# Fetched expert rows gated and added on GpSimd instead of VectorE, in a two-block transformer kernel

## The reference, cut to what matters

```python
def moe_swiglu(h, router, w_gate, w_up, w_down):
    ...
    vals, idx = lax.top_k(probs, TOP_K)
    wts = vals / jnp.sum(vals, axis=-1, keepdims=True)
    gates = jnp.einsum('tk,tke->te', wts, jax.nn.one_hot(idx, N_EXPERTS, dtype=jnp.float32)).astype(h.dtype)
    out = jnp.zeros_like(ht)
    for e in range(N_EXPERTS):
        out = out + gates[:, e:e + 1] * swiglu(ht, w_gate[e], w_up[e], w_down[e])
    return out.reshape(bsz, seq, d)
```

## Time and profile before

| | |
|---|---|
| Median of three runs | 1274.33 us (1272.78 to 1274.46) |
| The profiled execution, its time | 1270.87 us |
| Its span in the profile | 1269.1 us |
| Granted TensorE clock, mean over the span | 0.999 of full speed |
| TensorE busy | 1236.7 us (97%) |
| VectorE busy | 1001.9 us (79%) |
| ScalarE busy | 844.2 us (67%) |
| GpSimd busy | 39.0 us (3%), 47 instructions |

### The profile page before, as it was taken

How to read it: one execution, slowest core, us unless ns; L and a number is a source line. 1 busy time by engine, 2 the same in 40 slices (tenths; PEclk the granted TensorE clock), 3 DMA queues, 4 the chain that set the end, 5 groups by cost and what they waited for, 6 DMA issues and landing times.

```text
span 1269.1 us, 18118 instructions
## 1 busy us (share of the span) xinstructions
PE 1236.7 (97%) x5924; PEld 1015.1 (80%) x5924; DVE 1001.9 (79%) x1397; ACT 844.2 (67%) x1218; POOL 39.0 (3%) x47
## 2 busy tenths in 40 slices
PE   7999999999998999999999999999997999999998
PEld 6878888888777787888788888888786877888887
DVE  6577555556977899999999999999999787766664
ACT  5656444446755788888888888888886587544442
POOL 0000000000100000000000000000100121000000
PEclk9999999999999999999999999999999999999999
DMA  9744555554233699999999999989998433455540
GB/s 357 276 162 170 195 187 181 194 198 166 68 133 133 257 369 378 363 361 370 362 376 372 357 376 374 375 344 370 375 422 301 166 140 115 165 182 196 175 156 34
DMA packets 48196, 325.22 MB, mean 256 GB/s; under 512 B 5416, under 2 KB 6704, under 8 KB 9872
## 3 DMA queue, kind: packets, MB, share of 16 engines
q1 hardware_dynamic: 44704, 316.40, 66.4%
q10 hardware_dynamic: 2752, 5.77, 1.2%
q0 software_dynamic: 688, 2.36, 0.5%
HBM read 318.74 MB, written 5.77 MB: 256 GB/s over the span
## 4 chain that ended last, share of the span: by engine, by line
PE 89%; DVE 5%; ACT 3%; issue 1%; POOL 0%; DMA 0%; SPq 0%; DVEq 0%; ACTq 0%
PE bank L431 25%; PE bank L433 25%; PE bank L432 25%; PE bank L1135 4%; PE bank L1136 2%; DVE wl L1812 2%; PE bank L495 2%; ACT wh L1193 1%; PE bank L842 1%; PE bank L467 1%; PE bank L697 1%; PE bank L1134 1%; PE bank L696 1%; DMA x<-x_dram 0%; DVE xt L1832 0%
## 5 line engine op out<-in xcount | busy, mean ns | idle before, releaser
L1812 DVE TENSOR_TENSOR wl<-raw,wh 128x1024 fp32r<-128x1024 f32 x598 | 714.5, 1219 | 180.3 <-ACT wh L1193 170.3
L1193 ACT ACTIVATE wh<-raw 128x1024 fp32r<-128x1024 f32 x598 | 630.5, 1058 | 278.2 <-PE bank L433 239.5
L431 PE MATMUL bank<-wh,xt 128*128 128x512 f32 (+2 forms) x1026 | 406.4, 396 | 6.6 <-DVE xt L1832 2.5
L433 PE MATMUL bank<-wh,xt 128*128 128x512 f32 (+2 forms) x1026 | 397.1, 387 | 0.0
L432 PE MATMUL bank<-wl,xt 128*128 128x512 f32 (+2 forms) x1026 | 396.5, 386 | 0.0
L431 PEld LDWEIGHTS bank<-wh,xt 128*128 128x128 f32 x1026 | 193.1, 188 | 45.5 <-DVE xt L1832 3.2
L433 PEld LDWEIGHTS bank<-wh,xt 128*128 128x128 f32 x1026 | 192.9, 188 | 40.3
L432 PEld LDWEIGHTS bank<-wl,xt 128*128 128x128 f32 x1026 | 193.4, 189 | 36.1
L431 PE MATMUL bank<-wh,hth 128*128 128x512 f32 x472 | 186.4, 395 | 1.0 <-DVE htl L1880 0.4
L433 PE MATMUL bank<-wh,htl 128*128 128x512 f32 x472 | 184.7, 391 | 0.0
L432 PE MATMUL bank<-wl,hth 128*128 128x512 f32 x472 | 184.3, 390 | 0.0
(11 more groups left out here) (304 smaller groups left out, 822.6 us busy)
## 6 DMA issues: line engine op xcount, KB each, us to landing
raw<-weights_dram SPq DMA_DIRECT2D x299, 1024.0 KB, 5.2
expert_results<-wide ACTq DMA_DIRECT2D x7, 512.0 KB
x<-x_dram SPq DMA_DIRECT2D x2, 512.0 KB, 7.3
wide<-bias_scratch ACTq DMA_DIRECT2D x8, 128.0 KB, 4.0
out_dram<-x SPq DMA_DIRECT2D x4, 256.0 KB, 2.0
fixed<-fixed_dram SPq DMA_DIRECT2D x1, 536.0 KB, 11.2
bias_scratch<-act ACTq DMA_DIRECT2D x2, 256.0 KB, 8.5
bias_scratch<-hbuf ACTq DMA_DIRECT2D x2, 256.0 KB, 14.9
```

What stands on the lines that cost most here:

```text
L431: mm(o, lh, wh[:, wi, sl], start=start, stop=False)
L433: return mm(o, ll, wh[:, wi, sl], start=False, stop=stop)
L1193: A(wh[:, c % SPLIT, 0:n], raw[:, (c // 2) % RAW, (c % 2) * UNIT:(c % 2) * UNIT + n], ACT.Copy).then_inc(hi_done, 1)
L1812: V.tensor_tensor(wl[:, c % SPLIT, 0:n], raw[:, (c // 2) % RAW, (c % 2) * UNIT:(c % 2) * UNIT + n], f32(wh[:, c % SPLIT, 0:n]), ALU.subtra ...
```

## The change

The four fused operations of `add_fetched` on VectorE go, with the wait for the fetch and the hooks (`near_end`) by which they were called. On GpSimd, right behind the four indirect DMAs, eight operations of 128x1024 come in: four multiply the fetched rows by their gates in place, and four add them to x, one after the other for the same half of x. They count the semaphore `ob_rs` up to eight. VectorE waits for that count before `add_scattered`, and the waits of `scaled_ob` are raised by the same eight.

```diff
@@ gpsimd, behind the four indirect DMAs
+            pool.wait_ge(sem("fetched"), 64)
+            for choice in range(2):
+                for t in range(NT):
+                    gate = small[:, 68 + 2 * choice + t:69 + 2 * choice + t]
+                    g.tensor_scalar(fetched(choice, t), fetched(choice, t), gate, None, ALU.mult).then_inc(sem("ob_rs"), 1)
+            for choice in range(2):
+                for t in range(NT):
+                    pool.wait_ge(sem("ob_rs"), 2 * NT if choice == 0 else 2 * NT + t + 1)
+                    g.tensor_tensor(x[:, t, :], x[:, t, :], fetched(choice, t), ALU.add).then_inc(sem("ob_rs"), 1)
             norm_rs("attn2")
@@ vector, ffn
-                if near_end:
-                    near_end(0)
...
-                        if near_end:
-                            near_end(1)
@@ vector
-            def add_fetched(t):
-
-                dv.wait_ge(sem("fetched"), 64)
-                for choice in range(2):
-                    gate = small[:, 68 + 2 * choice + t:69 + 2 * choice + t]
-                    link(V.scalar_tensor_tensor(out=x[:, t, :], in0=fetched(choice, t), scalar=gate, in1=x[:, t, :],
-                                                op0=ALU.mult, op1=ALU.add))
-
             def add_scattered():
 
+                dv.wait_ge(sem("ob_rs"), 4 * NT)
                 for n in range(2):
...
-            expert(NE - 1, 2, near_end=add_fetched, leave=leave_moe)
+            expert(NE - 1, 2, leave=leave_moe)
@@ vector, scaled_ob
-                dv.wait_ge(sem("ob_rs"), h + 1)
+                dv.wait_ge(sem("ob_rs"), 4 * NT + h + 1)
```

More of the change, by code:

```diff
@@ L1853, in out_proj, with ffn @@
                 turned_lo(tag, range(4, 8), 6)
-            def ffn(tag, c0, nf, U, loops, width, nd, i0, f0=0, nt=NT, early=None, late=None, done=0, leave=None, middle=None, near_end=None):
+            def ffn(tag, c0, nf, U, loops, width, nd, i0, f0=0, nt=NT, early=None, late=None, done=0, leave=None, middle=None):
                 nj = width // P
```

## The result

The changed kernel is slower. Its median is 1275.61 us (18 runs, 1273.65 to 1281.09) against 1272.72 us of the kernel before (18 runs, 1271.12 to 1274.91); the ratio is 1.0026 with a 95% interval of 1.0018 to 1.0033. Its profiled execution took 1275.02 us, with a span of 1272.9. The prediction was 1280.6 us, or +6.3 us. The sign was right and 1275.61 lies in the range, but only about half of the forecast slowdown came: 2.9 us between the medians, 3.3 by the ratio. The absolute figure misses by 5.0 us. Some 1.6 of that is the base: the prediction started from the median of three runs, 1274.33, and that of eighteen is 1272.72.

The account below looks back on a forecast made before the run. TensorE, busy 97% of the span, was taken as the bound. New idle time of 10.7 us plus 1.5 us of low clock less 5.9 us for the removal gave +6.3 us, 1280.6 us; range 1268 to 1287.

Parts of the forecast that it names:

- What bounds the kernel: Whole kernel: TensorE busy 97% of the span; near the change it waits 4.6 us for VectorE's line 1870.
- what the removal gives: End of the mixture: without VectorE's four additions, 4.4 us of TensorE waiting and 1.5 us of slow clock go, 5.9 together.
- Two-sided hold: VectorE's splits beside GpSimd: each engine's operation holds the other's, a GpSimd operation for its whole length; 13.8 us held.
- H: Time GpSimd's eight operations hold VectorE's splits, from about 930 us on: 13.8 us, ends 9.2 and 24.
- (b): Rival on VectorE's splits: held, but only 5 to 10 us; net -2.5 to +2.5 us, middle 1274.3; chance 16%.
- What is absorbed: 930 to 955 us: 3.1 us of held time doesn't reach TensorE, so 10.7 come out as idle time.
- the low clock's cost: TensorE's products behind its last wait for VectorE run at 1.2 GHz instead of 2.4; 1.5 us, counted once.
- The margin of 1.3 us: VectorE's lead over TensorE: first additions put 2.59 us in and 1.26 came out, so 1.3 us is absorbed.
- H - 7.5: General net change in us for held time H; the change breaks even at 7.5 us held.
- When it runs: GpSimd's new work: last fetch lands at 930 us, work lasts until 953, VectorE's new wait costs nothing.
- (a): Rival on VectorE's splits: GpSimd waits for them but they aren't held; only the removal counts, -5.9 us, 1268.4; chance 20%.
- (c): Rival on GpSimd: served only when VectorE rests, so VectorE's new wait stalls TensorE; +7.5 us, 1281.8; chance 6%.

Follow-up runs that it names:

- the eight additions: Kernel before with eight further additions of 128x1024 on GpSimd in expert 0's steps; 1290.95 us, ratio 1.0136.
- the spread kernel: Kernel before with VectorE's four additions spread out, one behind line 1880 of each of steps 3 to 6 of expert 7; 1271.01 us, ratio 0.9988.
- the run for their own durations: Kernel before with one multiplication and one addition of 128x1024 on GpSimd near the start; multiplication 2.89 us, addition 2.36 us.

## Why the prediction was right or wrong

**What bounds the kernel, and what the removal gives: right.** 5.9 us were forecast, 5.7 shown by the run without additions, and the 0.2 us of waiting left over were 0.54.

**Two-sided hold: right.** It decided the sign. The rows of short operations showed only that GpSimd waits for splits; that splits wait for GpSimd was taken on argument and on the rule of the Trainium skill, and the eight additions show it. The Trainium skill, "SBUF — State Buffer", section "SBUF: two separate sides", has the one that starts first keep the shared interface for the whole instruction. That is nearly borne out for additions: held 1.9 to 2.1 us of the 2.36 that one takes. It isn't for multiplications: by this rule 2.89 us would be held each time, and 0.8 to 0.84 were.

**The held time: the term that failed.** I had H = 13.8 us: 4 x 2.3 for the additions and 4 x 1.15 for the multiplications. The additions held 8.45 us (9.2 forecast). The multiplications lengthened the groups of splits by 0.3 us at most instead of 4.6. Where their hold comes out whole it is 0.84 us each, 3.4 for four, so even then the term was too large; here it hid, and the run with multiplications alone is as fast as the run with none. So H was 8.7 us. That is below the 10 us on which my forecast rested and inside the 5 to 10 us of rival (b).

**What is absorbed: wrong too, the other way.** I took off 3.1 us. In the profiled execution the last two steps are 7.34 and 1.92 us longer than without additions. The last turn waits 0.54 us in both, so the 1.92 us are the slow products, the low clock's cost (1.5 forecast, from the one wait of 3.30 us), and the 7.34 are what came out of the 8.7 held: 1.4 were absorbed. The sum counted slack twice. The margin of 1.3 us was read from a step that already had its own 0.45 us of slack in it, and three more steps of slack were added, while the additions stood within a step and a half. The runs agree on 1.0 to 1.4 us: 1.2 for the first addition of the spread kernel, 1.1 (7.65 less 6.5) with additions only, 1.0 with two additions. On the low clock the runs show no simple rule. It came behind 7.18, 3.30 and 3.05 us of idle TensorE, and didn't behind 2.87 and 3.48 us.

Term by term: 13.8 - 3.1 + 1.5 - 5.9 = +6.3 was forecast, 8.7 - 1.4 + 1.9 - 5.7 = +3.5 came (3.6 in the table, by rounding). The errors partly cancel: the prediction's own rule, H - 7.5, gives only +1.2 us for H = 8.7. With that H alone put right the forecast would have been no clear change. With the absorption and the clock alone put right it would have been +8.6 us. That the sum came no further off is luck, and a range from 6 us below the base to 13 above it holds nearly every outcome of such a sum.

**When it runs: partly.** The rows landed at 936.4 in this execution, not 930; the upper bound of 3.0 us for an operation was broken by the multiplications' 4.2 and the additions' 3.15, which hold waiting for splits besides the 2.89 and 2.36 us of the run for their own durations. The additions therefore ran from 953 to 966 and put their waiting into one step, where I had it in 930 to 955. VectorE's new wait cost nothing, as forecast: it was fulfilled at 966.0, some 17 us ahead of the additions at 983.5.

**The rivals.** VectorE not held (a) is refuted by the splits of up to 3.4 us in the changed kernel, starvation (c) by the missing wait. Held but less (b), at 16%, is the case that came by its condition: H was 8.7 us. Its reasons were not quite the right ones (the additions were not as fast as VectorE's; the multiplications hid), and its net of 2.5 us at most came out too low because it took off the same 3.1 us.

## What to carry to other kernels

Before work goes to GpSimd beside a busy VectorE, ask how many of VectorE's instructions there read two operands from SBUF, and count the time of GpSimd's two-operand operations as VectorE's own: here an addition held VectorE for about 2 us, against 1.28 us for the fused operation that it replaced. Instructions with one operand are not safe by that alone: the two casts took two and three times as long. An instruction that is on the path is better cut up and placed where its engine already waits; the same four operations spread out gave 0.26% with nothing moved to another engine. GpSimd's multiplications, with one large operand, hid here while VectorE was on time and came out once it was late. And when slack is read from a row, take care not to add it again as slack of the same step.

## What the runs showed of the hardware that was not expected

- A multiplication of 128x1024 by a per-partition value on GpSimd takes 2.89 us with one short VectorE operation beside it, more than an addition of two tiles (2.36), yet it holds VectorE for only 0.84 us. Beside splits it stretches to between 4.1 and 4.8 us.
- The hold appears in VectorE's durations, not in its idle time: splits of up to 3.4 us in place of 1.22, so that VectorE's busy share rises while it does less.
- Additions cut in four held 5.8 us in all instead of 8.45, although GpSimd took 24.15 us for them instead of 12.59.
- Casts of 32x512 on VectorE with one operand in SBUF took 0.89 and 1.24 us beside memsets on GpSimd, and 0.41 us in the kernel before.
- An idle time of 3.05 us of TensorE was followed by the lower clock and one of 3.48 us was not.
